# A 32-step threshold search spread over ScalarE and VectorE: the search's update in four operations instead of six, with the sign moved into the scale operand of the counting activation

## The chip, the cores and the metric

The kernel runs on one core of one Trainium2 chip. The metric is the device time in microseconds (us) of one execution. TensorE, VectorE, ScalarE and GpSimd (PE, DVE, ACT and POOL in the rows) each run their own instruction stream in order and wait for each other by semaphores; SyncE issues the DMAs.

## The reference, cut to what matters

One decoder layer over 1,024 tokens of width 1,024: an input projection, then three groups of heads (a gated delta rule, a sparse attention over selected keys, a cross-attention into 256 memory tokens), an output projection and a LayerNorm. The change touches the selection of keys for the sparse attention. For each query the 256 keys with the highest score are kept:

```python
logits = jnp.einsum('bqjd,bsd->bqjs', qi, k_idx).astype(jnp.float32) * (IDX_DIM ** -0.5)
score = jnp.einsum('bqjs,bqj->bqs', jax.nn.relu(logits), wi.astype(jnp.float32) * (IDX_HEADS ** -0.5))
score = jnp.where(causal[None], score, -jnp.inf)
_, idx = lax.top_k(score, topk)          # topk = 256
```

Only the query blocks 2 to 7 (of 8 blocks of 128 queries) have more than 256 keys to choose from, so six blocks are searched.

## The kernel before, in words

Everything is in one order written out by hand, `make_plan()`: a list of events such as `("proj", h, part, t, s)` or `("count", it, b)`. Each engine walks the same list and issues its own part of every event. An engine's instructions thus have the order of the list, and a wait for one event holds up everything that stands behind it on that engine.

The selection finds, for each of the 6 blocks at once, the score of the 256th key by a search over the 32 bits of a float32. A step of the search (`it` = 0 to 31) has two parts:

- Six `count` events on ScalarE, one for each block b, of width (b+1)*128: an activation `Sign` over the block's scores (tile `score`) with the tried threshold as bias (a column of the tile `sel`, one value per query) and the sum of the signs as accumulated output, `n_low`. The step counts in pairs: blocks 7 and 2, 6 and 3, 5 and 4. In the rows a count is two instructions of L1697: the ACTIVATE `cst<-score,sel` and the ACTIVATION_READ_ACCUMULATOR behind it. The signs themselves go to two scratch areas of `cst` and are not used.
- One `update` event on VectorE, a few operations on 128x6 columns of `sel`, all in the rows as `sel<-sel`: L1323 (`n_off`, how far the count is from the wanted one), L1334 (`n_off` times `t_sign`), L1335 (`bit_kept`), L1337 (`bits_tried`, the bits found so far with the next one), L1339 (`candidate` = `bits_tried` times `t_sign`, which releases the next counts through `candidates_ready`), and behind the release L1340 (`bits`). `link` makes each operation wait until the one before has written.

Step 0 counts at threshold zero and finds the sign `t_sign` of each threshold; its update is L1323, L1327, L1328, L1329 and L1330.

The selection events are woven between the projections (L878, L879 and L880: three matmuls on split operands) and the four delta-rule heads. One head has a triangular inverse (L1021, L1034, L1047 and L1049) and then a scan over 8 blocks, whose steps alternate between TensorE (L1067, L1073, L1084, L1088, L1089) and VectorE: `vnew` (L1474), `dn_s` (L1482, L1484) and `oall` (L1243, L1246). The steps of the search stand between about 168 and 494 us of the span, beside the heads 0, 1 and 2. On ScalarE the same stretch holds the evacuations from PSUM (L1614, a copy helper), the SiLUs (L1731), the squares of the outputs (L1621) and, ahead of each scan, the key norms and decays (L1746, L1747, L1754); GpSimd multiplies the decays (L1872, L1877). After the search VectorE alone makes the masks (L1363 to L1519), and the attention and output projection of the 8 blocks follow.

Of the kernel before, what the change touches and what calls it, by code (L numbers as in the profile page):

```python
# [29 lines left out]
P = 128  # L30
# [7 lines left out]
TOPK = 256  # L38
# [36 lines left out]
U32 = mybir.dt.uint32  # L75
ALU = mybir.AluOpType
ACT = mybir.ActivationFunctionType
# [3 lines left out]
C_BIT = C_KT + SEQ  # L81
# [26 lines left out]
def score_at(b):  # L108

    return sum((i + 1) * P for i in range(2, b))  # L110
# [316 lines left out]
def build(nc, x, x_t, mem_t, w_groups, conv_t, dn_a_log, dn_dt_bias, dn_norm_w, kv_norm_w, wuk_t, w_uv, wmem_t, wout_t,  # L427
# [3 lines left out]
    with ctx:  # L431
        def sb(name, cols):
            return ctx.enter_context(nc.sbuf_tensor(name, [P, cols], F32))

        def sem(name):
            return ctx.enter_context(nc.semaphore(name))

        cst = sb("cst", C_ALL)
# [22 lines left out]
        score = sb("score", SCORE_W)  # L461
# [89 lines left out]
        def xs_of(b):  # L551
# [18 lines left out]
            sc32[:, i * 32:(i + 1) * 32] for i in range(16))  # L570
        css, crs = misc[:, 0:8], misc[:, 8:16]

        n_low, n_half, t_sign, n_off, bit_kept, bits, bits_tried, candidate, t_high, t_low = (
            sel[:, i * N_SEL:(i + 1) * N_SEL] for i in range(10))

        signs = [cst[:, C_KT + i * 512:C_KT + (i + 1) * 512].bitcast(BF16) for i in range(2)]
        eps_rms, eps_ln, one1 = misc[:, 16:17], misc[:, 17:18], misc[:, 18:19]
# [49 lines left out]
        candidates_ready = sem("candidates_ready")  # L627
        keys_counted = sem("keys_counted")
# [42 lines left out]
        order = {}  # L671
# [526 lines left out]
        def _(dve):  # L1198
            v = nc.vector
# [3 lines left out]
            def link(ins):  # L1203

                steps[0] += 1
                ins.then_inc(dve_chain, 1)
                dve.wait_ge(dve_chain, steps[0])
# [44 lines left out]
            v.memset(candidate, 0.0)  # L1252
            for b in range(2, NB):

                v.memset(n_half[:, b - 2:b - 1], (b + 1) * P - 2 * TOPK + 0.5)
            v.memset(eps_ln, LN_EPS).then_inc(small_constants_set, 1)
            for e in plan:
                k = e[0]
# [40 lines left out]
                elif k == "idx":  # L1299
                    b, j, c = e[1:]  # L1300
# [3 lines left out]
                    w = wis[:, b, j:j + 1]  # L1304
# [15 lines left out]
                elif k == "update":  # L1320
                    it = e[1]
                    dve.wait_ge(keys_counted, N_SEL * (it + 1))
                    link(v.tensor_tensor(n_off, n_low, n_half, ALU.subtract))  # L1323
                    if it == 0:

                        dve.wait_ge(bit_sem, 16)
                        link(v.tensor_scalar(t_sign, n_off, 0.0, 2.0, ALU.is_lt, ALU.mult))  # L1327
                        link(v.tensor_scalar(t_sign, t_sign, -1.0, None, ALU.add))  # L1328
                        v.memset(bits, 0.0)  # L1329
                        v.tensor_scalar(candidate, t_sign, 2.0, None, ALU.mult).then_inc(candidates_ready, 1)  # L1330
                    else:

                        bit = FLOAT_BITS - 1 - it
                        link(v.tensor_tensor(n_off, n_off, t_sign, ALU.mult))  # L1334
                        link(v.tensor_scalar(bit_kept.bitcast(U32), n_off, 0.0, float(1 << bit), ALU.is_lt, ALU.mult))  # L1335
                        if bit:
                            link(v.scalar_tensor_tensor(bits_tried.bitcast(U32), bit_kept.bitcast(U32), cst[:, C_BIT + bit - 1:C_BIT + bit].bitcast(U32),  # L1337
                                                        bits.bitcast(U32), ALU.bitwise_or, ALU.bitwise_or))
                            v.tensor_tensor(candidate, bits_tried, t_sign, ALU.mult).then_inc(candidates_ready, 1)  # L1339
                        link(v.tensor_tensor(bits.bitcast(U32), bits.bitcast(U32), bit_kept.bitcast(U32), ALU.bitwise_or))  # L1340
                        if bit == 0:

                            low, carry, up = bit_kept.bitcast(U32), n_off.bitcast(U32), bits_tried.bitcast(U32)
                            link(v.tensor_scalar(carry, bits.bitcast(U32), 16, None, ALU.logical_shift_right))
                            link(v.tensor_scalar(up, carry, 16, None, ALU.logical_shift_left))
                            link(v.tensor_tensor(low, bits.bitcast(U32), up, ALU.bitwise_xor))
                            link(v.tensor_scalar(low, low, 1.0, None, ALU.add))

                            link(v.tensor_scalar(carry, low, 16, None, ALU.logical_shift_right))
                            link(v.tensor_scalar(carry, carry, 16, None, ALU.logical_shift_left))  # L1350
                            link(v.tensor_tensor(low, low, carry, ALU.bitwise_xor))
                            link(v.tensor_tensor(up, up, carry, ALU.add))
                            link(v.tensor_tensor(up, up, low, ALU.bitwise_or))
                            link(v.tensor_tensor(bits, bits, t_sign, ALU.mult))
                            link(v.tensor_tensor(bits_tried, bits_tried, t_sign, ALU.mult))
                            v.tensor_tensor(t_high, bits, bits_tried, ALU.max)
                            link(v.tensor_tensor(t_low, bits, bits_tried, ALU.min))
                elif k == "reach":

                    b = e[1]  # L1360
                    one = slice(b - 2, b - 1)
                    w = (b + 1) * P
                    link(v.tensor_scalar(picked_above[:, 0:w], score[:, score_at(b):score_at(b + 1)], t_high[:, one], 0.0, ALU.is_ge, ALU.add,  # L1363
                                         accum_out=n_low[:, one]))
# [95 lines left out]
                elif k == "XY":  # L1460
                    h, a, s = e[1:]
                    w = 1 << s
# [7 lines left out]
                elif k == "scanV":  # L1470
                    h, b = e[1:]
# [3 lines left out]
                elif k == "scanS":  # L1475
                    h, b = e[1:]
# [20 lines left out]
                elif k == "dm":  # L1497
                    b, stage_ = e[1:]
                    w = (b + 1) * P
# [20 lines left out]
                elif k == "sc":  # L1520
                    b, h, c = e[1:]
# [13 lines left out]
                elif k == "msc":  # L1535
                    b, i = e[1:]
# [9 lines left out]
                elif k == "rinv":  # L1546
                    b = e[1]
# [8 lines left out]
                elif k == "o":  # L1556
                    b = e[1]
# [3 lines left out]
                elif k == "mix_split":  # L1561
                    b = e[1]
                    dve.wait_ge(mix_hi_ready, PLACE[b] + 1)
                    v.tensor_tensor(mix_lo[:, :], av(MIXT_AT, DM), mix_hi[:, :].bitcast(F32), ALU.subtract).then_inc(mix_split, 1)  # L1564
                elif k == "mixT":
                    b, i = e[1:]
# [8 lines left out]
                elif k == "y":  # L1575
                    b, i = e[1:]
# [12 lines left out]
                elif k == "ln":  # L1589
                    b = e[1]  # L1590
# [11 lines left out]
        def _(act):  # L1602
            sc = nc.scalar
# [3 lines left out]
            def link(ins):  # L1607

                steps[0] += 1
                ins.then_inc(act_chain, 1)  # L1610
                act.wait_ge(act_chain, steps[0])
# [22 lines left out]
            for e in plan:  # L1634
# [43 lines left out]
                elif k == "idx":  # L1678
                    b, j, c = e[1:]
# [6 lines left out]
                elif k == "count":  # L1686
                    it, b = e[1:]
                    w = (b + 1) * P
# [5 lines left out]
                    if order[e] > 2:  # L1694
                        act.wait_ge(keys_counted, order[e] - 2)

                    sc.activation(signs[order[e] % 2][:, 0:w], score[:, score_at(b):score_at(b + 1)], ACT.Sign, scale=-1.0,  # L1697
                                  bias=candidate[:, b - 2:b - 1], accum_out=n_low[:, b - 2:b - 1]).then_inc(keys_counted, 1)
                elif k == "gates":
                    act.wait_ge(gate_steps_by_dve, 1)  # L1700
                    for b in range(NB):
# [66 lines left out]
                elif k == "scanS":  # L1768
                    h, b = e[1:]
# [23 lines left out]
                elif k == "sc":  # L1793
                    b, h, c = e[1:]
# [4 lines left out]
                elif k == "msc":  # L1799
                    b, i = e[1:]  # L1800
                    act.wait_ge(mem_max_ready, 2 * PLACE[b] + i + 1)
                    for m in range(2):
                        g = 2 * m + i
                        last = sc.activation(mp[:, g * 256:(g + 1) * 256], ps(e)[:, m * 256:(m + 1) * 256], ACT.Exp, scale=0.125,
                                             bias=mmx[:, 2 * i + m:2 * i + m + 1], accum_out=sums[:, 4 + g:5 + g])
# [11 lines left out]
                elif k == "mixT" and e[2] == 1:  # L1817

                    b = e[1]
# [3 lines left out]
                elif k == "rstd":  # L1823
                    b = e[1]
# [157 lines left out]
```

## Time and profile before

| | |
|---|---|
| runs before | 853.98 us median of 3 (852.0 to 854.2) |
| profiled execution, its own time | 854.07 us |
| its span, first to last instruction | 852.3 us, mean granted TensorE clock 0.959 |
| TensorE matmuls busy | 765.4 us, 90% |
| VectorE busy | 495.9 us, 58% |
| ScalarE busy | 461.4 us, 54% |
| the 192 counts (L1697) on ScalarE | 166.8 us, and 36.6 us of accumulator reads |

A busy share says how long an engine had an instruction in work, not whether the end depends on it. For a small edit the rows of waits and the order of instructions around one wait say more.

### The profile page before, as it was taken

The page shows a single profiled execution, that of the slowest core. Times are in us where ns is not written, and L with a number is a line of the kernel's source. Part 1 is how long each engine was busy: PE and PEld are TensorE (multiplying, and loading weights), DVE is VectorE, ACT ScalarE, POOL GpSimd, SP SyncE. Part 2 cuts the span into 40 slices and gives each one's busy share as a digit, 9 for nine tenths or more (in the row PEclk, how much of TensorE's full clock was granted, in tenths as well). Part 3 has the DMA queues.
Part 4 walks back from the last instruction along what each step waited for, and adds up shares of the span by engine and source line. Part 5 has one row for each costly group of instructions (what it writes and reads, how often), then busy time and mean ns, then how long its engine had stood idle before and what let it go on. Part 6 is the DMA issues. An engine that isn't in the chain of part 4 may idle for free.

```text
span 852.3 us, 11425 instructions
## 1 busy us (share of the span) xinstructions
PE 765.4 (90%) x3996; PEld 622.0 (73%) x3996; DVE 495.9 (58%) x1068; ACT 461.4 (54%) x1045; POOL 152.3 (18%) x248
## 2 busy tenths in 40 slices
PE   6999969899997999989997999876698998998975
PEld 5888858777886788778886788663566776774764
DVE  5633868755655565564655487843556456636532
ACT  4433566789777975998778932233443333332310
POOL 0000000063112510233112610001003033302330
PEclk9999979999998999999998999997899999999998
DMA  9312110123201330023001231009102112120201
GB/s 358 103 50 75 49 38 26 37 66 103 65 26 56 75 104 25 27 77 106 26 26 56 74 116 50 36 28 349 58 1 74 44 56 87 67 63 33 75 25 49
DMA packets 56424, 60.87 MB, mean 71 GB/s; under 512 B 16048, under 2 KB 42928, under 8 KB 55984
## 3 DMA queue, kind: packets, MB, share of 16 engines
q1 hardware_dynamic: 56368, 60.15, 21.4%
q8 instruction: 32, 0.52, 0.3%
q14 instruction: 24, 0.20, 0.1%
HBM read 45.46 MB, written 14.68 MB: 71 GB/s over the span
## 4 chain that ended last, share of the span: by engine, by line
PE 58%; DVE 17%; ACT 14%; issue 8%; DMA 2%; SPq 1%; POOL 0%; DVEq 0%; ACTq 0%; POOLq 0%
PE bank L870 16%; PE bank L878 8%; PE bank L880 8%; PE bank L879 8%; ACT cst L1697 5%; PE bank L884 3%; PE bank L1114 2%; PE bank L1142 2%; PE bank L1034 2%; PE bank L1049 2%; PE bank L1021 2%; PE bank L1047 2%; ACT ring_split L1614 2%; DVE score L1317 1%; DVE mix_lo L1564 1%
## 5 line engine op out<-in xcount | busy, mean ns | idle before, releaser
L878 PE MATMUL bank<-x_hi,ring_split 128*128 128x512 f32 x480 | 199.6, 416 | 7.8 <-DVE x_lo L1262 7.3
L880 PE MATMUL bank<-x_hi,ring_split 128*128 128x512 f32 x480 | 191.1, 398 | 0.0
L879 PE MATMUL bank<-x_lo,ring_split 128*128 128x512 f32 x480 | 190.5, 397 | 0.0
L1697 ACT ACTIVATE cst<-score,sel 128x1024 bf16<-128x1024 f32 (+2 forms) x192 | 166.8, 873 | 24.0 <-DVE sel L1339 24.0
L878 PEld LDWEIGHTS bank<-x_hi,ring_split 128*128 128x128 f32 x480 | 92.4, 192 | 24.2 <-DVE ring_split L1270 7.9
L880 PEld LDWEIGHTS bank<-x_hi,ring_split 128*128 128x128 f32 x480 | 92.0, 192 | 20.3
L879 PEld LDWEIGHTS bank<-x_lo,ring_split 128*128 128x128 f32 x480 | 92.3, 192 | 15.2
L1798 ACT ACTIVATE arena<-arena,misc 128x512 f32<-128x512 f32 (+7 forms) x32 | 24.8, 775 | 80.9 <-DVE misc L1534 80.9
L1614 ACT ACTIVATE arena<-bank 128x512 f32<-128x512 f32 (+1 forms) x108 | 49.7, 499 | 34.5 <-PE bank L884 10.5
L870 PE MATMUL bank<-w_out_hi,mix_hi 128*128 128x512 f32 x128 | 56.4, 441 | 6.7 <-DVE mix_lo L1564 4.2
L1872 POOL TENSOR_TENSOR arena<-arena,hsc 128x512 f32<-128x512 f32 x8 | 9.2, 1149 | 275.9 <-ACT arena L1754 275.9
L1584 DVE SCALAR_TENSOR_TENSOR arena<-qkvT,bank 128x512 f32<-128x512 f32 x16 | 11.0, 687 | 81.6 <-PE bank L870 81.6
L1317 DVE SCALAR_TENSOR_TENSOR score<-arena,wis,score 128x384 f32<-128x384 f32 (+3 forms) x70 | 46.1, 658 | 11.8 <-ACT arena L1685 5.7
L884 PEld LDWEIGHTS bank<-cst,arena 128*128 128x128 f32 x320 | 39.2, 148 | 18.5 <-issue 9.2
L1859 POOL TENSOR_TENSOR arena<-arena,cst 128x512 f32<-128x512 f32 x24 | 33.5, 1416 | 106.9 <-DVE arena L1223 50.6
L1685 ACT ACTIVATE arena<-bank 128x384 f32<-128x384 f32 (+3 forms) x80 | 38.9, 524 | 25.1 <-DVE score L1317 19.7
L870 PE MATMUL bank<-w_out_lo,mix_hi 128*128 128x512 f32 x128 | 52.4, 409 | 0.0
L1114 PE MATMUL bank<-cT,arena 128*128 128x512 f32 (+5 forms) x96 | 40.8, 537 | 12.2 <-DVE misc L1528 10.4
L870 PE MATMUL bank<-w_out_hi,mix_lo 128*128 128x512 f32 x128 | 51.7, 404 | 0.0
L884 PE MATMUL bank<-cst,arena 128*128 128x128 f32 x320 | 47.2, 284 | 4.5 <-DVE arena L1439 3.2
L1270 DVE TENSOR_TENSOR ring_split<-ring,ring_split 128x1024 fp32r<-128x1024 f32 x30 | 38.3, 1276 | 7.4 <-ACT ring_split L1614 7.1
L1114 PEld LDWEIGHTS bank<-cT,arena 128*128 128x128 f32 x96 | 18.0, 201 | 32.3 <-DVE misc L1528 18.2
(246 smaller groups left out, 1453.4 us busy)
## 6 DMA issues: line engine op xcount, KB each, us to landing
ring<-in_w_groups SPq DMA_DIRECT2D x30, 512.0 KB, 3.5
x_raw<-in_x_t SPq DMA_DIRECT2D x8, 512.0 KB, 9.3
side_z<-stage SPq DMA_DIRECT2D x16, 256.0 KB, 2.0
w_out_sb<-in_wout_t SPq DMA_DIRECT2D x2, 2048.0 KB, 12.4
zgT<-side_z SPq DMA_DIRECT2D x8, 512.0 KB, 3.9
qkvT<-in_x SPq DMA_DIRECT2D x8, 512.0 KB, 4.8
out_y<-arena SPq DMA_DIRECT2D x8, 512.0 KB, 2.8
ring<-in_wmem_t SPq DMA_DIRECT2D x2, 1024.0 KB, 4.8
```

The source lines that it names most:

```text
L870: last = nc.tensor.matmul(dst, w, r, start=(i == 0), stop=(i == len(pairs) - 1))
L878: nc.tensor.matmul(dst, hi, xh, start=(c == 0), stop=False)
L879: nc.tensor.matmul(dst, hi, xl, start=False, stop=False)
L880: last = nc.tensor.matmul(dst, lo, xh, start=False, stop=(c == KT - 1))
L884: return nc.tensor.transpose(dst, src, ident[0:n, 0:n])
L1114: nc.tensor.matmul(ps(e)[:, 0:hi - lo], qab[:, h * P:(h + 1) * P], cT[:, lo:hi], start=True, stop=True).then_inc(fill_of(e), 1)
L1270: v.tensor_tensor(lo, whole, hi.bitcast(F32), ALU.subtract).then_inc(weights_split, 1)
L1317: last = v.scalar_tensor_tensor(score[:, at + lo:at + hi], r[:, 0:hi - lo], w, score[:, at + lo:at + hi], ALU.mult, ALU.add)
L1614: return sc.activation(dst, src, ACT.Copy, scale=scale)
L1685: sc.activation(rbuf[(order[e] - 1) % 3][:, 0:hi - lo], ps(e)[:, 0:hi - lo], ACT.Relu, scale=IXD ** -0.5).then_inc(release_of(e), 1)
L1697: sc.activation(signs[order[e] % 2][:, 0:w], score[:, score_at(b):score_at(b + 1)], ACT.Sign, scale=-1.0, bias=candidate[:, b - 2:b - 1], ...
L1859: g.tensor_tensor(quad(row(a, R_UO[s % 2])), quad(row(a, R_U)), rep(cst[:, C_LEV + s * P:C_LEV + (s + 1) * P], 4), ALU.mult).then_inc(leve ...
```

## The change

The tried threshold is a magnitude with a sign. Before, both the tried threshold and the count were multiplied by the sign in every step. After, the activation takes `bits_tried` itself as bias and the negated sign as its scale, which is now a column of `sel` (the tile's t_high part, free until the search ends) instead of the constant -1.0. The count then has the sign in it, so that `n_off` needs no product either, if the wanted count (`n_half`, now `n_wanted`) is multiplied by the sign once, in step 0. The update of steps 1 to 31 has L1334 and L1339 no more. The update of step 0 has more: the scale column, the product for `n_wanted`, and two memsets, in a chain of links. The counts of step 0 keep the constant scale. The plan is the same, and no other instruction of any engine changes or changes its place; lines behind L576 are two higher after.

```diff
-        n_low, n_half, t_sign, n_off, bit_kept, bits, bits_tried, candidate, t_high, t_low = (
+        n_low, n_wanted, t_sign, n_off, bit_kept, bits, bits_tried, candidate, t_high, t_low = (
             sel[:, i * N_SEL:(i + 1) * N_SEL] for i in range(10))
+
+        score_scale = t_high
...
                     dve.wait_ge(keys_counted, N_SEL * (it + 1))
-                    link(v.tensor_tensor(n_off, n_low, n_half, ALU.subtract))
+                    link(v.tensor_tensor(n_off, n_low, n_wanted, ALU.subtract))
                     if it == 0:
 
                         dve.wait_ge(bit_sem, 16)
                         link(v.tensor_scalar(t_sign, n_off, 0.0, 2.0, ALU.is_lt, ALU.mult))
                         link(v.tensor_scalar(t_sign, t_sign, -1.0, None, ALU.add))
-                        v.memset(bits, 0.0)
-                        v.tensor_scalar(candidate, t_sign, 2.0, None, ALU.mult).then_inc(candidates_ready, 1)
+                        link(v.tensor_scalar(score_scale, t_sign, -1.0, None, ALU.mult))
+                        link(v.tensor_tensor(n_wanted, n_wanted, t_sign, ALU.mult))
+                        link(v.memset(bits, 0.0))
+                        v.memset(bits_tried, 2.0).then_inc(candidates_ready, 1)
                     else:
 
                         bit = FLOAT_BITS - 1 - it
-                        link(v.tensor_tensor(n_off, n_off, t_sign, ALU.mult))
                         link(v.tensor_scalar(bit_kept.bitcast(U32), n_off, 0.0, float(1 << bit), ALU.is_lt, ALU.mult))
                         if bit:
-                            link(v.scalar_tensor_tensor(bits_tried.bitcast(U32), bit_kept.bitcast(U32), cst[:, C_BIT + bit - 1:C_BIT + bit].bitcast(U32),
-                                                        bits.bitcast(U32), ALU.bitwise_or, ALU.bitwise_or))
-                            v.tensor_tensor(candidate, bits_tried, t_sign, ALU.mult).then_inc(candidates_ready, 1)
+                            v.scalar_tensor_tensor(bits_tried.bitcast(U32), bit_kept.bitcast(U32), cst[:, C_BIT + bit - 1:C_BIT + bit].bitcast(U32),
+                                                        bits.bitcast(U32), ALU.bitwise_or, ALU.bitwise_or).then_inc(candidates_ready, 1)
                         link(v.tensor_tensor(bits.bitcast(U32), bits.bitcast(U32), bit_kept.bitcast(U32), ALU.bitwise_or))
...
-                    sc.activation(signs[order[e] % 2][:, 0:w], score[:, score_at(b):score_at(b + 1)], ACT.Sign, scale=-1.0,
-                                  bias=candidate[:, b - 2:b - 1], accum_out=n_low[:, b - 2:b - 1]).then_inc(keys_counted, 1)
+                    tried, scale = (bits_tried, score_scale[:, b - 2:b - 1]) if it else (candidate, -1.0)
+                    sc.activation(signs[order[e] % 2][:, 0:w], score[:, score_at(b):score_at(b + 1)], ACT.Sign, scale=scale,
+                                  bias=tried[:, b - 2:b - 1], accum_out=n_low[:, b - 2:b - 1]).then_inc(keys_counted, 1)
```

## Rows read from the trace of the kernel before

**Rows 1.** The page, chain that ended last, by engine.
```profile
PE 58%; DVE 17%; ACT 14%; issue 8%; DMA 2%; SPq 1%; POOL 0%; DVEq 0%; ACTq 0%; POOLq 0%
```

**Rows 2.** Busy time by stretch: length, then busy us of PE, PEld, DVE, ACT, POOL.
```profile
176.00:495.00 319.00, 301.29 (x1739) 261.40 (x1740) 186.36 (x455) 257.62 (x577) 88.55 (x166) 0.97 0.22 64
```

**Rows 3.** Waits of PE from 176 to 495 us: total us, times, longest.
```profile
PE bank L1084 <- DVE vnew L1474: 13.4, 6, 3.8
PE bank L1067 <- DVE oall L1246: 3.0, 5, 1.3
...
PE bank L878 <- DVE stage L1298: 0.3, 1, 0.3
```

**Rows 4.** Timeline of PE in the scan of head 0; idle time before in brackets.
```profile
259.37 0.49 PE L1084 MATMUL bank<-vnew,arena 128*128 128x128 f32 x2 [0.66 <-DVE vnew L1474]
267.98 0.80 PE L1084 MATMUL bank<-vnew,arena 128*128 128x128 f32 x2 [3.81 <-DVE vnew L1474]
295.75 0.49 PE L1067 MATMUL bank<-arena 128*128 128x128 f32 x2 [1.35 <-DVE oall L1246]
```

**Rows 5.** Timeline of DVE, one update and what stands behind it.
```profile
265.70 0.17 DVE L1323 TENSOR_TENSOR sel<-sel 128x6 f32<-128x6 f32 x1 [5.46 <-ACT cst L1697]
265.91 0.17 DVE L1334 TENSOR_TENSOR sel<-sel 128x6 f32<-128x6 f32 x1
266.11 0.17 DVE L1335 TENSOR_SCALAR sel<-sel 128x6 uint32<-128x6 f32 x1
266.31 0.23 DVE L1337 SCALAR_TENSOR_TENSOR sel<-sel,cst 128x6 uint32<-128x6 uint32 x1
266.57 0.17 DVE L1339 TENSOR_TENSOR sel<-sel 128x6 f32<-128x6 f32 x1
266.65 0.16 DVE L1340 TENSOR_TENSOR sel<-sel 128x6 uint32<-128x6 uint32 x1
266.85 0.75 DVE L1234 SCALAR_TENSOR_TENSOR qkvT<-hbuf,cw,qkvT 128x512 f32<-128x512 f32 x1
```

**Rows 6.** Timeline of ACT, the next count behind that update.
```profile
266.77 1.15 ACT L1697 ACTIVATE cst<-score,sel 128x1024 bf16<-128x1024 f32 x1 [1.10 <-DVE sel L1339]
```

**Rows 7.** Timelines of DVE and POOL around the update at 256.55 us.
```profile
257.28 0.97 DVE L1334 TENSOR_TENSOR sel<-sel 128x6 f32<-128x6 f32 x1
...
258.74 0.17 DVE L1339 TENSOR_TENSOR sel<-sel 128x6 f32<-128x6 f32 x1
...
257.18 1.04 POOL L1877 TENSOR_TENSOR arena<-arena,sc 128x512 f32<-128x512 f32 x1
```

**Rows 8.** L1697 by stretch: busy us (instructions; two are one count).
```profile
246.50:250.10 3.60, 3.57 (x8) 1.00 0.01 2
...
258.90:265.70 6.80, 5.39 (x12) 1.00 0.16 66
278.50:294.00 15.50, 10.80 (x24) 1.00 0.26 72
...
181.00:201.30 20.30, 14.27 (x32) 1.00 0.26 82
```

**Rows 9.** Groups of ACT by shape: count, busy us, mean ns, idle before.
```profile
L1614 ACT ACTIVATE oall<-bank,sc 128x128 f32<-128x128 f32 x28 | 10.0, 357 | 21.4 <-PE bank L1089 21.3
...
L1614 ACT ACTIVATE arena<-bank 128x128 f32<-128x128 f32 x32 | 6.3, 286 | 5.5 <-PE bank L1103 5.3
...
L1826 ACT ACTIVATE hsc<-hsc,misc 128x1 f32<-128x1 f32 x8 | 2.4, 294 | 51.9 <-DVE hsc L1588 51.9
...
L1827 ACT ACTIVATE hsc<-hsc 128x1 f32<-128x1 f32 x8 | 1.6, 203 | 0.3
```

**Rows 10.** Timeline of ACT behind the first counts of step 1.
```profile
179.79 0.60 ACT L1614 ACTIVATE hbuf<-bank 128x512 f32<-128x512 f32 x1 [1.37 <-PE bank L880]
```

**Rows 11.** PE by stretch around the long wait: busy us, then granted clock.
```profile
268.00:270.00 2.00, 2.00 (x8) 0.50 0.00 0
...
274.00:276.00 2.00, 2.00 (x16) 1.00 0.40 142
```

More of the change, by code:

```diff
@@ L1253, in _ @@
             for b in range(2, NB):
-                v.memset(n_half[:, b - 2:b - 1], (b + 1) * P - 2 * TOPK + 0.5)
+                v.memset(n_wanted[:, b - 2:b - 1], (b + 1) * P - 2 * TOPK + 0.5)
             v.memset(eps_ln, LN_EPS).then_inc(small_constants_set, 1)
```

## The prediction

> **What bounds the kernel now.** I read the chain of work that ended last first. PE carries 58% of it, DVE 17% and ACT 14% [rows 1]. That chain runs through many of the counts and updates, but it follows whatever came last, even by a hair, so it doesn't say what a faster update is worth. The stretches do: from 176 to 495 us, where steps 1 to 31 of the search lie, PE is busy for 301.29 of 319 us [rows 2]. No more than 17.7 us can be had there, and only where PE waits for something that hangs on the search. The list of PE's waits gives these: 13.4 us for `vnew`, 3.0 us for `oall` and 0.3 us for `stage` [rows 3], 16.7 us in all.
>
> The timeline shows their form in head 0: 0.66 us at 259.37, 3.81 us at 267.98 and 1.35 us at 295.75 [rows 4]. Heads 1 and 2 repeat it (six waits for `vnew` in three heads, the longest 3.8 us). The long one is read like this: DVE stands for 5.46 us at L1323, waiting for the last count of a step; then the update's six operations, a conv tap and at last `vnew` go by in order, though nothing but their place in the queue binds `vnew` to them [rows 5]. ACT in turn waits 1.10 us in each such step for the candidate [rows 6]. So before such a wait of PE, counts on ACT and updates on DVE stand in one chain. The reader should see that both are on it: a shorter update and a longer count pull against each other.
>
> **What is taken away: L1334 and L1339.** In the update at 265.70 the starts are 265.91 for L1334 and 266.11 for L1335, so L1334 takes 0.20 us with its link. L1337 starts at 266.31 and L1339 at 266.57, while the count starts at 266.77: L1339 takes 0.20 us [rows 5, 6]. What stands behind on DVE gains the same, since L1340 overlaps the operation in front of it either way (266.57 and 266.65 now, 266.31 and about 266.39 then) and the conv tap at 266.85 comes at about 266.45. So 0.40 us for an update that is on the chain, for ACT and DVE alike.
>
> The update ahead of the first wait of each head is another case. L1334 takes 0.97 us there, from 257.28 to 258.25, and a POOL product that reads SBUF runs from 257.18 to 258.22: it ends with it [rows 7]. The operation was held up, and taking it out doesn't take out what holds it. L1335 reads one tile, L1337 reads two, as L1334 does. I take it that L1335 passes and L1337 is held until POOL's end. Then the candidate is ready at about 258.3 instead of 258.91, when L1339 ends: 0.62 us. The bounds are 0.42 (L1335 is held too, then L1337 comes at full length) and 1.2 us (nothing is held).
> The Trainium skill, "SBUF — State Buffer", section "Who interferes with whom", says that a `tensor_tensor` with both inputs in SBUF contends with GpSimd's reads, and that the second to issue blocks until the first is done. The row on L1334 agrees, 0.97 us against 0.17.
>
> **What is added: a pointer in place of a constant, in 186 counts.** A count already has one column operand, the bias; now the scale is a second one. No row has both, so I bound the price p. Below: nothing, if both columns are fetched together. Nearest rows: a scale column on a copy of 128x128 from PSUM has 357 ns against 286 ns with constants, so 71 ns; a bias column has 294 against 203 ns on one element per partition, from SBUF, 91 ns [rows 9]. The count has the new kind of column but reads SBUF, so I take p = 0.082 us, between the two. Above: twice the bias column's price, 0.18 us, if two fetches hinder each other.
> The Trainium skill, "ScalarE: Activation LUTs", section "What ACT_TABLE_LOAD costs", states that each per-partition pointer operand adds about 93 ns. That speaks against the change: with 93 ns in the sum below, an estimate, the kernel comes out 1.0 us slower. The trace's 91 ns for the bias agrees; no row shows a second pointer.
>
> **The counts and updates on each chain.** From the last point at which ACT waited for PE's work:
> - To the second wait of a head (267.98): 4 counts before the table load and the decays, then the held update, then 6 counts and a plain update (x8 and x12 instructions) [rows 8]. The last two counts before the held update lie under POOL's products. Change: 10p - 0.62 - 0.40 = 10p - 1.02. The wait of 0.66 us at 259.37 lies on the same chain and isn't counted again.
> - To the end of the scan (295.75): behind the slow stretch PE hands over again; then come an update, 12 counts (x24) and an update [rows 8]. A third update lies under a table load and a SiLU on ACT. Change: 12p - 0.80. In head 1 this is two waits with half of it each, the sum is the same.
> - Ahead of these, the wait for `stage` (0.3 us): 16 counts (x32) and three updates [rows 8]. Change: 16p - 1.20.
>
> Three heads and the first chain: 3 x (22p - 1.82) + 16p - 1.20 = 82p - 6.66. With p = 0.082: **+0.1 us**. The rest of the 186 counts (and of the updates) lies where PE has other work and ACT waits for PE anyway, which takes up a tenth of a microsecond per count.
>
> **The rest at nothing.** The longer update of step 0 has two more linked operations of 0.2 us and two memsets, so step 1 starts about 0.5 us later; ACT then waits 1.37 us for PE at 179.79, which covers it [rows 10]. Uncovered it would cost 0.5 us. DVE has 59 fewer operations, some 10 us of busy time, but DVE isn't full. ACT has 186p = 15 us more work in a stretch where it was busy for 257.62 of 319 us [rows 2].
>
> **TensorE's clock.** Behind the long wait the granted clock is 0.50 (1.2 GHz) from 268 to 270 us and 1.00 (2.4 GHz) again from 274 [rows 11]. The 3.81 us of wait stays between 2.8 and 4.6 us in all cases, so I expect this three times as before. If the slow stretch begins or ends a microsecond or so elsewhere, half of that is gained or lost each time: +-1.5 us over three heads, in the range.
>
> **The sum.** The profiled execution took 854.07 us, 1.77 us over its span and 0.1 us above the median of the runs. 854.07 + 0.1 - 0.1 = 854.1 us.
>
> **Rivals.**
> - *The second pointer is free* (p below 0.02). Then the updates' gain stands alone: the two chains of a head give 1.02 and 0.80 us, and the first at most the 0.3 us of its wait: 3 x 1.82 + 0.3 = 5.8 us, 848.3 us. For it: the count is one instruction, and its first column may hide the second. Against: both columns have a price when alone [rows 9]. Chance 0.12.
> - *POOL no longer holds up the update, or the clock falls for less time.* With 1.2 instead of 0.62 us in three heads, 1.7 us more; with a shorter slow stretch 1.5 us more. Both together 3.2 us: 850.9 us. For it: L1334's 0.97 us is bound to POOL, not to its own work [rows 7]. Against: something that reads two tiles still follows. Chance 0.07.
> - *ScalarE becomes the bound* (the other side). If the two columns hinder each other, p = 0.18: 82 x 0.18 - 6.66 = +8.1 us, 862 us. It decides from p = 0.113 on, where the sum passes +2.6 us. For it: ACT is 81% busy there and every step's chain goes through its six counts; against: no row has so dear an operand. Chance 0.14.
> - *No change that can be told:* p between 0.05 and 0.113. 854.1 us. Chance 0.67.
>
> **How the numbers follow.** 0.3% of 854 is 2.6 us, about what a measurement of this kernel can tell from no change. Faster: 0.12 + 0.07 = 0.19. Slower: 0.14. Same: 0.67. The range goes from 848.5, nearly the free pointer's, to 857.5 (p = 0.125); outside lie most of the dear pointer's times and the edge of the free one's.
>
> **What would show it.** L1697's ACTIVATE of 128x1024 at about 1.23 us instead of 1.15, and ACT's wait behind an update down from 1.10 to 0.70 us. L1323 and L1335 back to back, two TENSOR_TENSORs gone. The three long waits of PE within 0.3 us of 3.8; the wait at the end of head 0's scan within 0.4 us of 1.35. In the held update the three-operand operation takes some 0.7 us. I am wrong if the counts have kept their length (then the kernel is faster), if they have grown by more than 0.113 us, or if PE waits at a place that isn't in the list.

## The result and the profile after

The changed kernel takes 854.55 us (median of 20 runs, 852.81 to 856.53), the kernel before 852.15 us in the 20 runs beside it. The ratio is 1.003, interval 1.0021 to 1.0039: 2.4 us slower, 1.8 to 3.3. That is inside the forecast range and just inside what was called no change.

The two profiled spans, 852.3 and 852.2 us, don't show it; why not is one of the questions below. The busy times of the changed kernel do show the exchange. From its page, the groups of L1700 (L1697 before):

```profile
L1700 ACT ACTIVATE cst<-score,sel 128x1024 bf16<-128x1024 f32 (+2 forms) x192 | 184.1, 963 | 15.9 <-DVE sel L1340 15.2
```

The counts were busy for 166.8 us before and are for 184.1 now: 17.3 us over the 186 counts of steps 1 to 31, 93 ns each. From 176 to 495 us, the stretch of [rows 2], the columns again length, then busy us of PE, PEld, DVE, ACT and POOL:

```profile
176.00:495.00 319.00, 299.85 (x1738) 260.00 (x1738) 174.96 (x393) 273.70 (x577) 87.13 (x166) 0.98 0.22 63
```

ACT has 16.1 us more work there, DVE 11.4 us less, and PE is busy for 1.4 us less. PE's waits of the same stretch answer to [rows 3]:

```profile
PE bank L1086 <- DVE vnew L1476: 13.8, 6, 4.0
PE bank L1069 <- DVE oall L1248: 3.8, 3, 1.7
...
PE bank L880 <- DVE stage L1300: 0.5, 1, 0.5
```

18.1 us against 16.7: the waits on the search have grown by 1.4 us. PE's timeline in head 0 (start, length, instruction, idle time before) answers to [rows 4]:

```profile
259.43 0.49 PE L1086 MATMUL bank<-vnew,arena 128*128 128x128 f32 x2 [0.63 <-DVE vnew L1476]
268.20 0.80 PE L1086 MATMUL bank<-vnew,arena 128*128 128x128 f32 x2 [3.96 <-DVE vnew L1476]
296.07 0.49 PE L1069 MATMUL bank<-arena 128*128 128x128 f32 x2 [1.66 <-DVE oall L1248]
```

All three waits have stayed, the second 0.15 and the third 0.31 us longer. The update is shorter by just what was forecast. DVE's timeline, against [rows 5], and ACT's next count, against [rows 6]:

```profile
266.33 0.17 DVE L1325 TENSOR_TENSOR sel<-sel 128x6 f32<-128x6 f32 x1 [6.01 <-ACT cst L1700]
266.53 0.17 DVE L1338 TENSOR_SCALAR sel<-sel 128x6 uint32<-128x6 f32 x1
266.74 0.23 DVE L1340 SCALAR_TENSOR_TENSOR sel<-sel,cst 128x6 uint32<-128x6 uint32 x1
266.88 0.16 DVE L1342 TENSOR_TENSOR sel<-sel 128x6 uint32<-128x6 uint32 x1
267.07 0.75 DVE L1236 SCALAR_TENSOR_TENSOR qkvT<-hbuf,cw,qkvT 128x512 f32<-128x512 f32 x1
...
267.00 1.24 ACT L1700 ACTIVATE cst<-score,sel 128x1024 bf16<-128x1024 f32 x1 [0.70 <-DVE sel L1340]
```

ACT's wait is 0.70 instead of 1.10 us, and the conv tap comes 0.74 us after the start of L1325, where it came 1.15 us after L1323. But DVE's wait for the counts is 6.01 instead of 5.46 us: six counts, each 0.093 us longer, take 0.56 us, more than the 0.40 us that the update gives.

The update that GpSimd holds up is another matter. DVE and then POOL at the place of [rows 7]:

```profile
257.20 0.51 DVE L1325 TENSOR_TENSOR sel<-sel 128x6 f32<-128x6 f32 x1 [0.21 <-ACT cst L1700]
257.74 0.97 DVE L1338 TENSOR_SCALAR sel<-sel 128x6 uint32<-128x6 f32 x1
258.75 0.23 DVE L1340 SCALAR_TENSOR_TENSOR sel<-sel,cst 128x6 uint32<-128x6 uint32 x1
...
257.65 1.04 POOL L1880 TENSOR_TENSOR arena<-arena,sc 128x512 f32<-128x512 f32 x1
```

L1338, which reads one tile only, now is the operation that lasts until POOL's product ends (257.65 + 1.04 = 258.69). It has 0.97 us, as L1334 had. From the end of POOL's product to the release of the next count 0.69 us went by before (258.22 to 258.91) and 0.29 us go by now (258.69 to 258.98). The held update gives 0.40 us, the lower bound of the prediction (0.42) and not its 0.62.

### The profile page after: what moved, and what is told of

The parts are those of the page before. It is cut to its first block, busy times and chain, and to the rows that moved or that the text cites. A ratio compares the mean times of both kernels' runs of the same rounds, so it can differ in the third digit from the quotient of the medians.

```text
span 852.2 us, 11366 instructions
## 1 busy us (share of the span) xinstructions
PE 763.5 (90%) x3996; PEld 620.2 (73%) x3996; DVE 484.9 (57%) x1009; ACT 478.1 (56%) x1045; POOL 150.9 (18%) x248
## 4 chain that ended last, share of the span: by engine, by line
PE 60%; DVE 15%; ACT 14%; issue 8%; DMA 2%; SPq 1%; POOL 0%; DVEq 0%; ACTq 0%; POOLq 0%
PE bank L872 15%; PE bank L880 8%; PE bank L882 8%; PE bank L881 8%; ACT cst L1700 5%; PE bank L886 3%; PE bank L1116 2%; PE bank L1144 2%; PE bank L1036 2%; DVE score L1319 2%; PE bank L1051 2%; PE bank L1049 2%; PE bank L1023 2%; ACT ring_split L1616 1%; DVE mix_lo L1566 1%
## 5 line engine op out<-in xcount | busy, mean ns | idle before, releaser
L1700 ACT ACTIVATE cst<-score,sel 128x1024 bf16<-128x1024 f32 (+2 forms) x192 | 184.1, 963 | 15.9 <-DVE sel L1340 15.2
L1687 ACT ACTIVATE arena<-bank 128x384 f32<-128x384 f32 (+3 forms) x80 | 39.0, 524 | 25.1 <-DVE score L1319 19.9
L1272 DVE TENSOR_TENSOR ring_split<-ring,ring_split 128x1024 fp32r<-128x1024 f32 x30 | 38.2, 1273 | 7.4 <-ACT ring_split L1616 7.1
```

Source lines behind the costliest of these rows:

```text
L1272: v.tensor_tensor(lo, whole, hi.bitcast(F32), ALU.subtract).then_inc(weights_split, 1)
L1687: sc.activation(rbuf[(order[e] - 1) % 3][:, 0:hi - lo], ps(e)[:, 0:hi - lo], ACT.Relu, scale=IXD ** -0.5).then_inc(release_of(e), 1)
```

## The experiments

The first question was whether the two halves of the change act as the sum has them: 82 counts and the updates of the chains. With the counts' measured growth of 0.093 us and the held update at 0.42 us, the forecast's sum becomes 82 x 0.093 - 6.06 = +1.6 us. The rival was that both halves are hidden and the 2.4 us come from somewhere else.

**The column alone.** The kernel before, with one column of -1.0 as scale.

```diff
+            v.memset(t_high, -1.0)
...
-                    sc.activation(..., ACT.Sign, scale=-1.0,
+                    sc.activation(..., ACT.Sign, scale=t_high[:, b - 2:b - 1] if it else -1.0,
```

> The kernel before with one thing added: the counts of steps 1 to 31 take their scale from a column that holds -1.0, in place of the constant. The update keeps its six operations. Theory A (82 counts lie on the chains that PE waits for, each grown by what the profile after showed, 17.3 us over 186 counts or 0.093 us): 82 x 0.093 = 7.6 us slower, ratio 1.009; the three long waits of PE grow by 10 x 0.093 = 0.93 us each, from 3.8 to 4.7 us. Rival B (the counts' growth is hidden, the changed kernel is slower because its update or the clock's slow stretches lie otherwise): within 2.5 us of before.

Measured: 863.3 us against 851.39, ratio 1.0144 (1.0123 to 1.0164), 11.9 us slower. PE's waits from 176 to 500 us:

```profile
PE bank L1084 <- DVE vnew L1475: 16.2, 6, 4.4
PE bank L1067 <- DVE oall L1246: 6.1, 6, 1.9
PE bank L878 <- DVE stage L1299: 1.7, 1, 1.7
```

24.0 us, 7.3 more than before, where theory A had 7.6: the vnew waits by 2.8 (30 counts of 0.093 us), the oall waits by 3.1 (36 counts give 3.3) and the stage wait by 1.4 (16 counts give 1.5). So each kind of wait grew about as the number of counts on its chain says. The longest wait itself grew by 0.6 us and not by 0.93. The short wait ahead of it lies on the same chain and took the rest: in head 0 it went from 0.66 us to 1.04 us in the second profile of this kernel. Rival B is out. But the time in the runs grew by 4.6 us more than the waits.

**The short update alone.** The changed kernel, with the constant scale; it leaves out the sign of the threshold.

```diff
-                    tried, scale = (bits_tried, score_scale[:, b - 2:b - 1]) if it else (candidate, -1.0)
+                    tried, scale = (bits_tried if it else candidate), -1.0
```

> The changed kernel with one thing undone: the counts keep the constant scale -1.0. It leaves out the sign of the threshold, so that for queries whose threshold is negative other keys are selected; no time hangs on the data. Theory A: the updates' gain alone, 0.40 us for a plain one and 0.42 for the one held by POOL, 3 x (0.82 + 0.80) + at most 0.3 = 5.2 us faster, ratio 0.994; the long waits of PE come to 3.8 - 0.8 = 3.0 us. Rival B (what the updates give is hidden behind other work): within 2.5 us of before. If A holds for both this and the column alone, the two sum to the change.

Measured: 847.76 us against 851.39, ratio 0.9961 (0.9946 to 0.9976), 3.6 us faster. PE's waits:

```profile
PE bank L1086 <- DVE vnew L1476: 11.0, 6, 3.4
PE bank L1069 <- DVE oall L1248: 1.5, 3, 0.6
```

12.5 us, 4.2 less than before, where 5.2 were expected: vnew 2.4 (three times 0.82, as expected), oall 1.5 and stage 0.3. The longest wait came to 3.4 us and not to 3.0; the short one ahead of it, 0.27 us in head 0, took the rest. For oall, 2.4 us were expected, and in head 0 the wait did give its 0.8 us (1.35 to 0.58). In the heads 1 and 2 the two waits before (0.46 and 0.38, 0.33 and 0.52 us) have become one each, of 0.50 and 0.47 us: they gave 0.34 and 0.38 us of 0.80. The reason is on ACT. In head 1 it now waits for PE inside this chain, where before it came late and didn't wait; what the shorter updates ahead of that point gave is lost there. The row of this kernel, then that of the kernel before:

```profile
374.75 0.60 ACT L1673 ACTIVATE stage<-bank 128x512 f32<-128x512 f32 x1 [0.42 <-PE bank L882]
378.23 0.60 ACT L1671 ACTIVATE stage<-bank 128x512 f32<-128x512 f32 x1
```

The column's cost has no such limit. So the halves don't add: the waits of the two alone give 7.3 - 4.2 = +3.1 us, together they give +1.4. If all of it had been passed on, the short update would have given 2.4 + 2.4 + 1.2 = 6.0 us, and 7.3 - 6.0 = 1.3.

**The changed kernel once more,** to see how far a result holds.

> The changed kernel once more, unchanged, on the same chip as the others. Theory A: 82 x 0.093 - 6.06 = +1.6 us, ratio 1.002; measured in the 20 runs: +2.4 us, ratio 1.003. Its profile shows a third set of positions of the slow clock behind the long waits: if these move the span, it will differ from the first profile of this kernel by up to 1.5 us at 512 us although no instruction has another length.

Measured: 853.93 us, ratio 1.0025 (1.0011 to 1.0038). Its waits are 13.8, 4.0 and 0.5 us, and the span is 851.6 us, 0.6 less than in the first profile.

**A dose between.** The column on three of the six counts.

```diff
+            v.memset(t_high, -1.0)
...
-                    sc.activation(..., ACT.Sign, scale=-1.0,
+                    sc.activation(..., ACT.Sign, scale=t_high[:, b - 2:b - 1] if it and b in (7, 6, 5) else -1.0,
```

> The kernel before with the scale column (holding -1.0) on three of the six counts of each of the steps 1 to 31, those of blocks 7, 6 and 5, one of each pair; the other three keep the constant. Theory A (each count on a chain that PE waits for passes its growth on in full, 0.093 us): half of the 82 counts, 41 x 0.093 = 3.8 us of waits of PE, half of what the column on all six gave (7.3 us in PE's waits); the long waits grow by 0.47 us each, to 4.3 us. Rival B (the growth is passed on only beyond some slack): less than 2.5 us of waits. Rival C (the two runs' times differ by more than PE's waits because longer waits bring more time at the slow clock): the time in the runs grows by more than the waits do.

Measured: 857.39 us against 851.62, ratio 1.0066 (1.0045 to 1.0087), 5.8 us slower. PE's waits:

```profile
PE bank L1084 <- DVE vnew L1475: 14.8, 6, 4.1
PE bank L1067 <- DVE oall L1246: 4.1, 5, 1.6
...
PE bank L878 <- DVE stage L1299: 1.0, 1, 1.0
```

19.9 us, 3.2 more than before, where 3.8 were expected; vnew (1.4) and stage (0.7) are as worked out, oall is short by 0.6. So the waits go nearly in step with the dose, and again the runs grow by more, 5.8 us (3.8 to 7.4). That is what rival C expects of the time; whether its cause, the slow clock, is the right one is looked at below.

**The kernel before, a second profile.**

> The kernel before once more, unchanged, for a second profile of it. Its first profiled execution took 854.07 us, 2.7 us above the median of its runs on this chip. Theory A (the clock's slow stretches behind the same waits begin and end elsewhere from execution to execution): PE's waits come out the same within 0.3 us in all, and the span differs as the time lost at the lower clock does. Rival B: the waits themselves differ between executions.

Measured: 851.74 us, ratio 0.9998 (0.9986 to 1.0009). Its waits are 13.4, 3.0 and 0.2 us, as in the first profile; the span is 850.7 us, 1.6 less. But the reason was not as simple as theory A: PE had 1.6 us more wait for ACT at the first L1021 and 1.5 us for DVE at 210.9 us, in exchange for less time at the slow clock.

**The column once more,** to see what the rest of 4.6 us is.

> The kernel of the scale column alone (update of six operations) once more, unchanged. Its runs were 11.9 us above those of before, its waits of PE in the search 7.3 us. Theory A (the rest is time at the slow clock, which differs between executions): the same 7.3 us of waits within 0.3 us, and a median nearer to 8 us above before. Rival B (the rest hangs on the column): the same 12 us in the runs, and a place in the profile, the same in both, where more than the listed waits is lost.

Measured: 862.2 us against 852.18, ratio 1.012 (1.0101 to 1.014), 10.0 us slower; PE's waits 16.2, 6.2 and 1.8 us. The waits repeat to 0.2 us. The 10.0 us lie between theory A's 8 and rival B's 12, and the intervals of the two measurements overlap, so the runs decide for neither. The groups of L1021 show the length of the search's stretch, as their first and last start: of the kernel before, of the column in its two profiles.

```profile
L1021 PE MATMUL bank<-arena,qkvT x96: 270/275/422, 176.3 to 492.4; 128*128 128x128 f32 x96
```

```profile
L1021 PE MATMUL bank<-arena,qkvT x96: 271/275/421, 178.4 to 502.0; 128*128 128x128 f32 x96
```

```profile
L1021 PE MATMUL bank<-arena,qkvT x96: 270/275/421, 176.8 to 500.6; 128*128 128x128 f32 x96
```

316.1 us in the first profile of the kernel before, 323.6 and 323.8 with the column: 7.5 and 7.7 us. That it meets the 7.6 of the sum so closely is partly luck, since this first profile is one of the longer ones: against the mean of four, 315.2 us (below), it is 8.4 and 8.6 us. In the first profile of the column another 2.1 us were lost before 178.4 us, where no count with a column stands yet (the first starts at 178.62 us); in the second only 0.5.

**More profiles of both kernels,** one execution each.

> The kernel before, one more profile, to see from where the time between executions comes. Theory A (position and number of the stretches at the slow clock): head to the first L1021, stretch to the last L1021, and tail each keep their length within 0.3 us except by slow clock, and the stretch is 316.1 us as in both earlier profiles.

> The changed kernel, one more profile. Theory A: PE's waits on the search 18.1 us as in both earlier profiles; the stretch from the first to the last L1023 is between 316 and 318 us, and what it has over 316.1 beyond the waits' 1.4 us is slow clock. Rival B: the 2.4 us of the runs lie outside the stretch, in the tail.

> As the other profile of the kernel before in this call: stretch 316.1 us by theory A; another length shows that a single profile of it is no measure of a microsecond.

> As the other profile of the changed kernel in this call: PE's waits on the search 18.1 us, the stretch 316 to 318 us.

The times were 850.57 and 851.12 us for the kernel before, 853.96 and 853.88 us for the changed one. PE's waits were 13.4, 3.0 and 0.3 us in both of the former, 13.8, 3.9 (and 4.0) and 0.5 us in the latter. The stretch from the first to the last L1021 (L1023) took, in the order of the four profiles of each kernel, 316.1, 316.1, 314.9 and 313.6 us before, mean 315.2, and 316.3, 316.2, 316.6 and 316.3 us after, mean 316.35. The spans were 852.3, 850.7, 848.8 and 849.3 us before, mean 850.3, and 852.2, 851.6, 852.2 and 852.1 after, mean 852.0. The forecast of 316.1 us for the kernel before was thus missed in both of these profiles. Of the 1.7 us between the mean spans, 1.15 lie in this stretch, and 0.75 behind it: from the last L1021 (L1023) to the end it is 359.9, 357.6, 357.7 and 359.1 us before and 359.3, 359.2, 359.5 and 359.4 us after. So rival B of the changed kernel's third profile has a part in it. PE's waits in this tail are the same (38.2 to 38.8 us in all eight).

What differs most between the executions of one kernel is the clock, in the search's stretch the clock behind the three long waits. PE by stretch (busy us, instructions, granted clock) in the third profile of the kernel before, then the second of the column:

```profile
255.00:280.00 25.00, 20.54 (x105) 0.86 0.19 56
350.00:375.00 25.00, 20.54 (x110) 0.93 0.17 54
445.00:475.00 30.00, 25.54 (x139) 0.94 0.18 55
```

```profile
255.00:280.00 25.00, 19.60 (x104) 0.93 0.17 53
350.00:375.00 25.00, 19.60 (x104) 0.86 0.07 23
445.00:475.00 30.00, 24.59 (x132) 0.89 0.10 32
```

The 25 us stretches show 0.93 or 0.86. Against full speed (1.2 instead of 2.4 GHz for a part of the stretch) that is 1.75 or 3.5 us of work. PE loses this at most, since the clock may fall while PE still waits. In the changed kernel PE stands still until 268.20 us, and its clock is already down on the way there, 0.70 in the 2 us in which PE is busy for 0.00 us:

```profile
266.00:268.00 2.00, 0.00 (x0) 0.00 (x0) 1.53 (x6) 1.30 (x3) 0.00 (x0) 0.70 0.00 0
268.00:270.00 2.00, 1.80 (x7) 1.78 (x8) 1.70 (x5) 2.00 (x7) 0.00 (x0) 0.50 0.00 0
```

In the four profiles before, the heads 0 and 1 and the third stretch up to 470 us have 0.86, 0.93, 0.86; 0.86, 0.93, 0.93; the same; and 0.93, 0.93, 0.93. The four of the changed kernel have 0.86, 0.93, 0.93 each time. That is also the mean of the kernel before, so these three stretches don't make the changed kernel slower.

**The update in integer bits.** The threshold keeps its sign bit, so that no product is needed, and the scale stays a constant.

```diff
+                    if it > 1:
...
+                            link(v.tensor_scalar(ahead, candidate.bitcast(U32), one_bit(last_bit - 1), one_bit(last_bit - 2), ALU.bitwise_xor, ALU.bitwise_or))
...
-                        link(v.tensor_tensor(n_off, n_off, t_sign, ALU.mult))
-                        link(v.tensor_scalar(bit_kept.bitcast(U32), n_off, 0.0, float(1 << bit), ALU.is_lt, ALU.mult))
+                        link(v.scalar_tensor_tensor(bit_kept.bitcast(U32), n_off.bitcast(U32), minus, flip, ALU.bitwise_and, ALU.bitwise_xor))
+                        shifted_in = (bit_kept.bitcast(U32), FLOAT_BITS - 1 - bit, ahead, ALU.logical_shift_right, ALU.bitwise_or)
                         if bit:
...
-                            v.tensor_tensor(candidate, bits_tried, t_sign, ALU.mult).then_inc(candidates_ready, 1)
-                        link(v.tensor_tensor(bits.bitcast(U32), bits.bitcast(U32), bit_kept.bitcast(U32), ALU.bitwise_or))
+                            v.scalar_tensor_tensor(candidate.bitcast(U32), *shifted_in).then_inc(candidates_ready, 1)
```

> Another way to an update of four operations, three of them between the last count and the next candidate, with the constant scale kept: the threshold's sign bit stays in the integer, the sign of the count is compared by bitwise and and xor, and the bits for the next step are prepared ahead of the wait for the counts. The whole computation is kept. Theory A: L1334, L1335, L1337, L1339 (0.20 + 0.20 + 0.26 + 0.20 = 0.86 us) become two three-operand operations of 0.26 us, so 0.34 us less for ACT and about 0.42 for what stands behind on DVE, where L1340 is gone too; in steps where DVE comes late the prepared operation costs 0.2 us. With the same chains about 3 x (0.76 + 0.76) + 0.3 = 4.9 us faster, ratio 0.994. Rival B: within 2.5 us.

Measured: 847.86 us against 851.39, ratio 0.996 (0.9945 to 0.9975): 3.5 us faster than before, and 6.1 us faster than the changed kernel on the same chip. PE's waits, then DVE at one update and ACT's next count:

```profile
PE bank L1084 <- DVE vnew L1487: 11.0, 6, 3.5
PE bank L1067 <- DVE oall L1246: 2.3, 3, 0.8
...
264.54 0.17 DVE L1335 TENSOR_TENSOR sel<-sel 128x6 f32<-128x6 f32 x1 [5.52 <-ACT cst L1710]
264.74 0.23 DVE L1347 SCALAR_TENSOR_TENSOR sel<-sel,cst 128x6 uint32<-128x6 uint32 x1
265.00 0.17 DVE L1350 SCALAR_TENSOR_TENSOR sel<-sel 128x6 uint32<-128x6 uint32 x1
...
265.20 1.15 ACT L1710 ACTIVATE cst<-score,sel 128x1024 bf16<-128x1024 f32 x1 [0.76 <-DVE sel L1350]
```

13.3 us of waits, 3.4 less than before. The vnew waits gave 2.4 us, as theory A has it (2.3); the oall waits gave 0.7 of 2.3 us, and so the whole is 3.4 and not 4.9 us. The path to the candidate is 0.66 us, and the count has its old length of 1.15 us. The stage wait is gone. The runs alone (2.1 to 4.7 us faster) don't exclude rival B's 2.5 us; the waits speak for A's chains.

**The column on top of the bits.** The same kernel with a column of -1.0 (in `bits`, which is free until the last step) as scale.

```diff
+            v.memset(bits, -1.0)
...
-                    sc.activation(..., ACT.Sign, scale=-1.0,
+                    sc.activation(..., ACT.Sign, scale=bits[:, b - 2:b - 1] if it else -1.0,
```

> The kernel with the update in integer bits, with one thing added: the counts of steps 1 to 31 take their scale from a column that holds -1.0. Theory A (a count's growth of 0.093 us is passed on through 82 counts, but waits that the short update had already emptied must first be filled again): the waits for vnew grow by 30 x 0.093 = 2.8 us, from 11.0 to 13.8; those for oall by 2 to 3.3 us from 2.3; that for stage by 0.3 at most; 5 to 6.4 us in all, so in the runs between 1.5 and 3 us above before, close to the changed kernel. Rival B (column and update are two separate costs that add): the 11.9 us of the column alone less the 3.5 us of this update, 8.4 us above before.

Measured: 857.84 us against 852.18, ratio 1.0056 (1.0041 to 1.0072), 5.7 us slower. The waits are as theory A has them, 13.8, 4.1 and 0.4 us, 5.0 more than without the column and 0.2 more than in the changed kernel. The time is not: it is between A's 3 and B's 8.4 us. In its profile head 0 and head 1 both have 0.86 behind the long wait, where the changed kernel has 0.86 and 0.93 with waits as long.

**Runs, waits and clock side by side.** The span and the mean granted clock were taken for nearly every execution, so the rest that the waits don't explain can be held against the clock. The last column is an estimate: the span times what the mean clock lacks to 1.0, averaged over the executions, less the same of the kernel before (for the changed kernel 31 executions against 55, for the others those beside them). It is uncertain by 0.4 us for the changed kernel and by up to 1.2 us for the others. It also counts slow clock while PE waits, which costs nothing.

| kernel | runs, us against before | PE's waits | rest | clock's shortfall, us |
|---|---|---|---|---|
| changed | +2.4 | +1.4 to +1.6 | +0.9 | +1.1 |
| column alone | +11.9 | +7.3 | +4.6 | +3.9 |
| column alone, again | +10.0 | +7.5 | +2.5 | +5.7 |
| column on three counts | +5.8 | +3.2 | +2.6 | +2.4 |
| short update alone | -3.6 | -4.2 | +0.6 | +0.4 |
| integer bits | -3.5 | -3.4 | -0.1 | +1.4 |
| integer bits with column | +5.7 | +1.6 | +4.1 | +4.9 |

The kernels with a large rest are those with a large shortfall. So the rest is, for the most part, slow clock; why the kernels with the column have more of it is not shown.

## Why the prediction came out as it did

**What bounds the kernel: right.** The waits listed as 16.7 us were the ones that moved, in every experiment, and the counts and updates of each chain were counted right: 7.3 to 7.5 us of waits for 7.6 worked out with the column alone, 2.4 for 2.46 in the vnew waits with the short update alone. In the changed kernel, with the two prices as measured, the chains give 3 x (10 x 0.093 - 0.82) = +0.33, 3 x (12 x 0.093 - 0.80) = +0.95 and 16 x 0.093 - 1.20 = +0.29 us, and the waits for vnew, oall and stage grew by 0.4, 0.8 to 1.0 and 0.2 us.

**The removed operations: right for a plain update, too good for the held one.** 0.40 us a plain update, for ACT and for DVE. The step that failed was that L1335 passes and L1337 is held: it is L1335, under its new number L1338, that is held (0.97 us in each of the three heads), and the gain is about the lower bound, 0.42 us (0.40 by the rows), in place of 0.62. Three heads: 0.6 us. The Trainium skill, "SBUF — State Buffer", section "Who interferes with whom", allows for this: a `tensor_scalar` whose operands meet the conditions can run in a mode that takes both ports, and then it contends with GpSimd; the prediction cited the page only for the product. The trace agrees, 0.97 us against 0.17 for the same operation elsewhere.

**The price of the pointer: too low.** It was taken as 0.082 us and is 0.093. At 82 counts that is 0.9 us. By the Trainium skill's 93 ns ("ScalarE: Activation LUTs", section "What ACT_TABLE_LOAD costs") the estimate was the better one, and the row of the counts now agrees with it for a second pointer beside the first. The scale row from PSUM, 71 ns, pulled the value down; the bias row on SBUF, 91 ns, was the nearer one.

With these two terms corrected the sum is +1.6 us, and the waits measured +1.4 to +1.6.

**The rest at nothing: right.** The longer update of step 0 made ACT wait 0.35 us at its first count, and ACT's wait for PE at 179.79 absorbed it.

**The clock: named, but its part was placed only in the width of the range.** The forecast expected the same slow stretches three times as before, +-1.5 us. One execution of the kernel before differs from another by just that, and the changed kernel's profiles all have the same clock behind the long waits. The third profile of the kernel before has it too, and its stretch is shorter than the changed kernel's mean by 316.35 - 314.9 = 1.4 us, the waits' growth. (So has the second, whose 316.1 us hold the 1.5 us of wait at 210.9 us.) The measured 2.4 us thus are 1.4 to 1.6 us of waits and a rest of about 0.9 us. This rest the prediction didn't have; by the table it is slow clock (1.1 us), and by the profiles most of it lies behind the search (0.75 us), where the counts are over and where the prediction didn't look. Four profiles don't settle a mean to 1 us. The first pair of profiles showed no difference because the kernel before was caught at 854.07 us, 1.9 us above its median of 20.

**The number: near by luck.** The forecast of 854.1 us is 0.45 us from the measured 854.55. But it was built on that one execution of 854.07 us. The change itself was forecast at +0.1 us and measured at +2.4: the starting point was 1.9 us too high and the change 2.3 us too low, and the two nearly cancel. "No change" holds by a hair, too, since the interval of 1.0021 to 1.0039 reaches past the 0.3% that the prediction drew as its border.

**What stays open.** The rest beyond the waits goes with the slow clock, but what brings the slow clock on was not shown. With the column alone the rest is 4.6 and 2.5 us, and against the mean of the kernel before its two profiles have some more slow clock in every part of the span, ahead of the search too. For the integer bits the shortfall is 1.4 us larger and the rest is nothing, so the two don't go together to the microsecond. For the changed kernel, why the part behind the search has the longer of its two forms in all four profiles, and in the kernel before only in two of four, is open as well.

## What to carry to other kernels

An operand that turns from a constant into a column is a cost in every instruction that has it: here 93 ns six times a step, to save two operations of 0.20 us once a step. Before moving work into an instruction that runs more often, multiply the saving and the cost by how often each stands on the chain that somebody waits for. Look first for a form that needs neither: a sign that stays in the bits cost no product and no column in the counts and gave 3.5 us. What a removed operation is worth ends where the wait that it shortens is gone, or where the shortened engine comes to wait for something else. What an added one costs has no such end, so two halves measured apart don't add. And take the starting point of a forecast from the median of many runs, not from the execution that happened to be profiled.

## What the runs showed of the hardware that was not expected

A column operand seems to have its price on VectorE as well. In the kernel with integer bits, the operation that prepares the next bits has two columns and 283 ns (median of 29), where L1335 of the kernel before, also one tile in and constants only, has 172 ns; the one with a single column has 229 ns. That is 54 to 57 ns each. Of the three-operand operations of the same kernel, L1347 with a column has 225 ns and L1350 without one 165 ns. The compared operations differ in their arithmetic too, and no run changed the column alone. The row of the operation with one column (busy us, mean ns), and the lines of the others (least, median and greatest ns):

```profile
L1343 DVE TENSOR_SCALAR sel<-sel,cst 128x6 uint32<-128x6 uint32 x1 | 0.2, 229 | 0.0
```

```profile
L1331 DVE TENSOR_SCALAR sel<-sel,cst x29: 279/283/1258, 190.2 to 476.4; 128x6 uint32<-128x6 uint32 x29
L1347 DVE SCALAR_TENSOR_TENSOR sel<-sel,cst x31: 224/225/299, 185.3 to 487.1; 128x6 uint32<-128x6 uint32 x31
L1350 DVE SCALAR_TENSOR_TENSOR sel<-sel x30: 165/165/269, 185.6 to 479.7; 128x6 uint32<-128x6 uint32 x30
```

What the clock costs behind one long wait differed between executions of the same kernel, and the wait's length alone didn't set it. Behind the first long wait of the kernel before the mean clock of the 25 us was 0.86 in three of four executions and 0.93 in the fourth, with the same 3.8 us of wait. With the column the wait was 4.4 us, and it was 0.93 in both.
